# The first block's weights: half of them by ScalarE's queue, and a wait in SyncE's

## The reference, cut to what matters

```python
def hybrid_mixer(x, w_in, lower_bound, ...):
    proj = x @ w_in                     # (256, 1024) @ (1024, 7168)
    q, f_pre, i_val, o_gate, pool_v, gate_a, gate_b = jnp.split(proj, splits, axis=-1)
    f = lb + (1.0 - lb) * jax.nn.sigmoid(f_pre)
    ...                                 # a gated recurrence, pooling, gates, projections
def reference(x, ...):
    x = first_block(x, ...)             # hybrid_mixer, layer norm, MLP 1024 -> 4096 -> 1024
    return second_block(x, mem, ...)    # attention, gating, cross attention, and last
                                        # an expert layer that gathers 128 rows a token
```

## Time and profile before

| | us |
|---|---|
| median of three runs | 1292.64 |
| lowest and highest of them | 1290.21, 1294.09 |
| the profiled execution | 1290.23 |
| its span, first to last instruction | 1288.5 |

### The profile page before, as it was taken

One profiled execution on the slowest core, in us unless ns is written; L12 is line 12 of the kernel. 1 busy time (PEld: TensorE's weight loads), 2 busy tenths in 40 slices (PEclk: granted clock), 3 DMA queues, 4 the chain that ended last, 5 costly groups with the idle time before them and its releaser, 6 DMA issues.

```text
span 1288.5 us, 16356 instructions
## 1 busy us (share of the span) xinstructions
PE 1182.6 (92%) x5734; PEld 830.3 (64%) x5734; DVE 928.5 (72%) x1855; ACT 556.5 (43%) x1018; POOL 296.4 (23%) x264
## 2 busy tenths in 40 slices
PE   9999999999999999999999989999987878777776
PEld 9988999888888899998855544554532323332322
DVE  6886758788854785586787787767667777777655
ACT  5833565466533556556445333322332222222323
POOL 0000000000000000000244455444554444544430
PEclk9999999999999999999999999999999998999999
DMA  7544455455555653466899999999999999999996
GB/s 290 186 174 139 163 214 207 163 194 195 203 211 191 212 195 133 164 241 249 329 421 419 419 420 419 419 420 419 419 421 419 420 420 420 420 420 420 419 420 269
DMA packets 56212, 396.14 MB, mean 307 GB/s; under 512 B 6352, under 2 KB 6352, under 8 KB 9296
## 3 DMA queue, kind: packets, MB, share of 16 engines
q0 software_dynamic: 37152, 268.45, 50.4%
q1 hardware_dynamic: 17136, 119.17, 25.7%
q10 hardware_dynamic: 1856, 7.60, 1.7%
HBM read 394.15 MB, written 1.05 MB: 307 GB/s over the span
## 4 chain that ended last, share of the span: by engine, by line
PE 61%; DMA 29%; DVE 4%; issue 2%; ACT 2%; POOL 1%; DVEq 0%; ACTq 0%; POOLq 0%
DMA R<-experts,IDX 27%; PE ps L650 12%; PE ps L1288 11%; PE ps L782 10%; PE ps L695 9%; PE ps L698 5%; PE ps L719 3%; DMA R<-experts,lb 2%; PE ps L732 2%; PE ps L662 2%; PE ps L1114 2%; DVE R L2813 1%; ACT DIAG L1820 1%; PE ps L829 1%; PE ps L818 1%
## 5 line engine op out<-in xcount | busy, mean ns | idle before, releaser
L1288 PE MATMUL ps<-R,DIAG 128*128 128x512 f32 x1020 | 480.5, 617 | 92.8 <-ACT DIAG L1820 92.2
L1288 PEld LDWEIGHTS ps<-R,DIAG 128*128 128x128 f32 x1020 | 189.6, 195 | 356.0 <-issue 196.1
L3038 POOL DMA_INDIRECT R<-experts,IDX x254 | 289.7, 1141 | 515.9 <-PE ps L1288 284.1
L2813 DVE CUSTOM_DVE_ANT_0 R<-R,XN 128x1024 f32<-128x1024 f32 x256 | 312.7, 1226 | 131.7 <-DMA R<-experts,IDX 130.8
L1966 DVE TENSOR_TENSOR w_lo<-raw,w_hi 128x1024 fp32r<-128x1024 f32 x192 | 227.4, 1220 | 70.9 <-ACT w_hi L1347 66.8
L1347 ACT ACTIVATE w_hi<-raw 128x1024 fp32r<-128x1024 f32 x191 | 192.9, 1052 | 69.4 <-DMA raw<-weights 68.2
L1802 ACT ACTIVATE act_d<-dots,rst 128x2 f32<-128x2 f32 (+1 forms) x132 | 39.0, 296 | 304.2 <-DVE dots L2813 304.0
L1820 ACT ACTIVATE DIAG<-con,coef 128x128 f32<-128x128 f32 x253 | 88.0, 394 | 121.8 <-DVE coef L2822 120.5
L695 PE MATMUL ps<-both_C,w_hi 128*128 128x512 f32 x384 | 134.4, 396 | 1.3 <-DVE both_C L1936 1.3
L698 PE MATMUL ps<-both_C,w_lo 128*128 128x256 f32 x384 | 106.9, 278 | 0.0
L3014 POOL TENSOR_SCALAR_AFFINE_SELECT WS<-WS 128x1024 f32<-128x1024 f32 x1 | 1.1, 1124 | 436.4 <-DMA BS<-gbs 436.4
(11 more groups left out here) (437 smaller groups left out, 1775.1 us busy)
## 6 DMA issues: line engine op xcount, KB each, us to landing
raw<-weights SPq DMA_DIRECT2D x95, 1024.0 KB, 4.8
PQW<-weights SPq DMA_DIRECT2D x8, 1024.0 KB, 7.1
R<-experts,IDX POOLq DMA_INDIRECT x254, 29.9
raw<-weights SPq DMA_DIRECT2D x4, 512.0 KB, 8.7
LNR<-rows ACTq DMA_DIRECT2D x2, 1024.0 KB, 4.7
early_raw<-weights SPq DMA_DIRECT2D x2, 1024.0 KB, 6.9
XQ<-weights SPq DMA_DIRECT2D x2, 1024.0 KB, 7.8
XO<-weights SPq DMA_DIRECT2D x2, 1024.0 KB, 11.0
```

Source lines behind the costliest of these rows:

```text
L1288: mm = pe.matmul(psum[:, 4 + 2 * m + n, :], DIAG[:, k, :], rows_[:, D + n * 512:D + (n + 1) * 512], start=(it % 8 == 0 and k == 0), stop=True,
L2813: dve.tensor_tensor_reduce(out=rows_[:, 0:D], in0=rows_[:, 0:D], in1=XN[:, m, :], scale=1.0, scalar=0.0, op0=ALU.mult, op1=ALU.add, accum_ ...
L3038: pool.indirect_dma_start(out=R[u][:, :], out_offset=None, in_=experts, in_offset=bass.IndirectOffsetOnAxis(ap=IDX[:, it, k:k + 1], axis=0 ...
```

## The change

The load of block 0's half 0 is taken out of SyncE's list and put at the start of ScalarE's program, ahead of its first wait, so that it goes through ScalarE's DMA queue. SyncE's order is then input half 0, input half 1, weights block 0 half 1; before the next issue (block 1's half 0) it waits until input half 0 has landed. What is computed, which bytes are loaded and the semaphores that others wait for are the same.

```diff
--- before.py
+++ after.py
@@ -585,9 +585,9 @@
                              weights[b][:, 1024 * h:1024 * h + 1024]).then_inc(signal, 16)
 
             load_x(0)
-            load_half(0, 0, first_in)
             load_x(1)
             load_half(0, 1, raw_ready[0])
+            sp.wait_ge(x_in[0], 16)
             load_half(1, 0, second_in)
             load_half(1, 1, raw_ready[1])
             sp.dma_start(vec[:, :], vecs).then_inc(vec_in, 16)
@@ -1353,6 +1353,8 @@
                 act.activation(w_hi[0][:, ks, :], raw[0][:, ks, :], ACT.Copy
                                ).then_inc(hi_ready if p % 2 else first_hi, 1)
 
+            act.dma_start(raw[0][:, 0:4, :].rearrange("p a b -> p (a b)"),
+                          weights[0][:, 0:1024]).then_inc(first_in, 16)
             for h in range(2):
                 ks = slice(4 * h, 4 * h + 4)
                 act.wait_ge(x_in[h], 16)
```

## The result

| | median us | lowest to highest | ratio to before |
|---|---|---|---|
| before, 22 runs | 1290.78 | 1289.41 to 1294.09 | |
| changed, 22 runs | 1293.45 | 1291.26 to 1294.68 | 1.0016, 95% interval 1.0010 to 1.0022 |

The change costs 2.1 us by the ratio (1.3 to 2.8 by its interval); the two medians themselves are 2.7 us apart. The forecast was no change within 0.3%, with a shift of +1.5 us, and 1292.9 us in a range of 1290.2 to 1296.0. The profiled execution went from 1290.23 to 1291.58.

A forecast was written before the change was run, and what follows sets the result against it. The start was taken as bound by warm-ups and data meeting within 0.1 us; the input 2.2 us later less 0.74 slack costs 1.5 us, which on 1291.4 gives 1292.9 us, range 1290.2 to 1296.0.

The forecast's parts named there:

- An even split of two queues, the input at 7.4: Start: input half 0 and weights half 0 share transfers evenly, so the input is usable at 7.4, not 5.17, 2.2 us later.
- Slack of 0.74 us, first matmul at 10.6: Start: input may come 0.74 us later for nothing; first matmul 10.6 instead of 9.12, cost 2.2 - 0.74 = 1.5 us.
- No bandwidth by the second queue: Start: loads from two engines interleave on the same 16 DMA engines, so the input and weights pair isn't sooner.
- The shift passes through: After the first matmul: dependent work and the gather move too, so the 1.5 us reach the end.
- The wait costs nothing, since block 1 lands as before: SyncE's wait for input half 0: block 1 issued at about 7.5, packets by 8.6, no hole in the stream, cost nothing.
- the cover that the text gave for the case of a miss: Block 1 behind SyncE's wait: were it 0.5 us late, it would still be split by 15.5, before 16.4.
- Rival 1: Start: the pause in SyncE's issues speeds early transfers; cost 0.2 us, no change, 1290.4; chance 0.27.
- Rival 2: Start: ScalarE's table load precedes its issue, so weights are issued at 2.1; cost 0.9 us; chance 0.1.
- Rival 3: TensorE's clock falls after the gap from 9.2 to 10.6, losing 2.9 us, 4.4 with the gap; chance 0.08.
- Had both loads come at 5 us, the warm-ups would still end at 9.22: Start, limit of any gain: the first matmul could come at most 0.1 us sooner, so no real gain.
- the base, taken as the middle of four times: Whole kernel: the shift was put on 1291.4, the middle of 1290.21, 1290.23, 1292.64 and 1294.09, giving 1292.9.

The follow-up runs named there:

- half the rival load: Changed kernel with only the first weight quarter on ScalarE's queue, the second behind input half 0 on SyncE's, wait kept: ratio 1.0019 (1.0008 to 1.0029).
- order-kept kernel: Against before: chunks 0 and 1 of input half 0, then weights half 0, through SyncE's queue, chunks 2 and 3 of each through ScalarE's: 1.0003 (0.9994 to 1.0012).
- queue-only kernel: Changed kernel without SyncE's wait for input half 0, the weights load staying on ScalarE's queue: ratio 1.0015 (1.0006 to 1.0024).
- quarters with fewer warm-ups: Before with block 0's input and weights loaded in quarters in TensorE's order on SyncE's queue, 8 warm-ups for 11: 0.9987, second time 0.9994.
- 8 warm-ups: Changed kernel with 8 in place of 11 warm-up matmuls, results unused: ratio 1.0020 (1.0011 to 1.0028), median 1294.04 us.

## Why the prediction was right, point by point

- **An even split of two queues, the input at 7.4.** Right: 7.51, and 0.44 and 0.48 MB in 2 to 6 us. Undoing the wait left the input at 7.43 and the time where it was; undoing the queue, or keeping the order over two queues, took the price away. The even split is one of packets, which were equally long here. Whether the bytes alone set the arrival is less sure: with half the rival load the input came 0.5 us sooner and not 1.0.
- **Slack of 0.74 us, first matmul at 10.6.** Right: 10.64 in the first profile, 10.55 in the second. The order-kept kernel used 0.5 of that slack for nothing.
- **No bandwidth by the second queue.** The Trainium skill ("DMA: Bandwidth & Descriptors", section "Issuing engines are not separate DMA queues") says that loads of different engines run on the same 16 DMA engines and interleave. The trace agrees: 229 GB/s by two queues, 221 by one.
- **The shift passes through.** Right: 1.51 us at 350 us, 1.35 in the profiled time. The ratio of all runs says 2.1, of which the start accounts for 1.5.
- **The wait costs nothing, since block 1 lands as before.** The cost was right, the reason wrong. Block 1 was picked up at 13.55 and not 11.99. I had the stream without a hole, with packets 1 us after the issue at 7.5; it moved 304 GB/s in 9 to 12 us where it moved 414 without the wait. What hid it was the cover that the text gave for the case of a miss: the low half was done at 15.9, and TensorE, itself 1.5 late, wanted it at 10.64 + 5.8 = 16.4. The wait had made block 1 2.1 us later (11.42 without it), and 0.5 us of slack were left. That the cover was long enough was partly luck, since the forecast had tried a delay of 0.5 us only.
- **Rival 1, the pause speeds transfers up.** Didn't happen: 229 GB/s with the pause, 233 without it (3 to 6 us of the queue-only kernel).
- **Rival 2, the table load first.** Didn't happen: issue at 0.83, table load at 1.27.
- **Rival 3, the clock.** It wasn't in either profile of the changed kernel, but it is a real mechanism of this place, one step further: 1.5 us, not the 2.9 that I took from the start-up, after gaps of 2.30 and 4.03 us. The trace of before had it too, after gaps of 1.88 to 2.76 us from 806 us on, and could have given that size: each fall lasts 3.5 to 4 us at half the pace. The prediction shows one gap of 1.30 us only. The Trainium skill ("TensorE: Matmul & The Clock Gate", "What's actually happening") says that an idle array goes back to half the clock; these rows agree, though not every such gap in them did it.
- **"Had both loads come at 5 us, the warm-ups would still end at 9.22."** Wrong, and with it the denial of any real gain. One execution's end of the warm-ups was taken for a fixed one; it lies between 7.7 and 9.2. Before is held by its data at 9.1 to 9.2 even where the warm-ups end at 7.74, and quarters with fewer warm-ups brought the first matmul 0.4 to 1.1 us forward.
- **The numbers.** The median of 1293.45 was forecast as 1292.9. That this is so close is partly luck: the base, taken as the middle of four times, 1291.4, is 1290.8 by 22 runs, 0.6 too high, and the shift between the medians, 2.7, is 1.2 more than the forecast's 1.5 (0.6 more by the ratio).

## What to carry to other kernels

A second DMA queue didn't add bandwidth here, it took away the order: put on it only what is needed at the same time as what is on the first, and look for the slack of each transfer in the waits of the engine behind it. Warm-up work that ends close to the data is a coincidence of one execution until several profiles show it; it pays to keep TensorE's idle time behind it short, as the clock fell after 2.30 and 4.03 us of it here and after none of 1.54 us or less, and between these the length alone doesn't tell. A wait in the issuing queue is cheap as long as what stands behind it has more slack than the hole that it makes, here 2.1 us of hole with 0.5 us to spare.

## What the runs showed of the hardware

- At the start TensorE's granted clock fell to 0.50 not in the gap but 0.6 to 1.0 us into the work behind it (8 warm-ups; one weight quarter), and stayed for some 3.5 us (10.10 to 11.1 at full pace, then 0.56, 0.50, 0.50, 0.73 by microsecond), for 1.5 us in all. In the expert stage of before one fall, at 1089.1, came 0.5 us before the work.
- The length of the gap alone doesn't decide it: before shows falls after 1.88 us (1074.49) and 2.00 us (805.65), and none after 2.00 us (927.29) and 2.65 us (1049.69).
- Two queues took turns by packet: 54 and 50 packets of equal length in 3 to 5 us of the changed kernel (0.22 and 0.20 MB), and 73 and 76 with one weight quarter, where ScalarE's were half as long (0.29 and 0.15 MB).
- At the start the granted clock reads 1.00 while the pieces run at half pace; there only their count tells the level.
- Two executions at a granted clock of 1.00 and without idle time ran one stage at paces 1.7% apart (463 against 455 matmuls in 80 us). What decides it is open.
